# A piece of the projections between the second and the third group of turned probabilities

## The reference

```
h = rmsnorm(x, norm_g)
proj = h @ w_in
ya = forgetting_attention(qa, ka, va, log_f) * silu(za)   # 8 heads, causal
yb = dsa_attention(qb, k, v, q_idx, k_idx, w_idx) * silu(zb)   # 8 heads, top 256 keys
yc = dilated_attention(qc, kc, vc) * silu(zc)   # 12 heads, short windows
merged = sigmoid(ga) * (ya @ w_a) + sigmoid(gb) * (yb @ w_b) + sigmoid(gc) * (yc @ w_c)
out = rmsnorm(x + merged @ w_o)
```

## Time and profile before

| what | value |
|---|---|
| median of 3 runs | 1521.58 us (1520.7 to 1522.74) |
| the profiled execution: time, span | 1528.18 us, 1526.2 us |
| TensorE busy | 1440.7 us, 94% of the span |
| VectorE, ScalarE busy | 727.6 us (48%), 695.9 us (46%) |
| DMA | mean 63 GB/s |
| granted clock of TensorE, mean | 0.982 |
| stage A (steps a0.0 to a3.7) | from 725.9 us in the span |
| stage B (steps b0.0 to b3.7) | from 972.3 us to about 1235 us |

### The profile page before, as it was taken

How to read it: one execution, slowest core, us unless ns; L and a number is a source line. 1 busy time by engine, 2 the same in 40 slices (tenths; PEclk the granted TensorE clock), 3 DMA queues, 4 the chain that set the end, 5 groups by cost and what they waited for, 6 DMA issues and landing times.

```text
span 1526.2 us, 20911 instructions
## 1 busy us (share of the span) xinstructions
PE 1440.7 (94%) x7890; PEld 1132.0 (74%) x7890; DVE 727.6 (48%) x1568; ACT 695.9 (46%) x1482; POOL 64.8 (4%) x133
## 2 busy tenths in 40 slices
PE   4978899999999999999999999999999999999898
PEld 3756667777776778887777777777777778888686
DVE  5363865545565894555434334543333346232524
ACT  6253666656675452111555565454544433211412
POOL 1102210000000000000000000100000000000000
PEclk9987999999999999999999999999999999999999
DMA  5115511111111112222111000312222221222422
GB/s 169 26 30 136 132 50 34 35 35 29 35 35 36 35 42 62 76 76 76 43 29 28 22 22 15 117 49 52 88 70 73 87 84 42 69 83 83 145 83 97
DMA packets 112131, 96.58 MB, mean 63 GB/s; under 512 B 10528, under 2 KB 97952, under 8 KB 111776
## 3 DMA queue, kind: packets, MB, share of 16 engines
q1 hardware_dynamic: 100816, 58.54, 14.4%
q0 software_dynamic: 11216, 36.71, 7.7%
HBM read 72.95 MB, written 18.09 MB: 60 GB/s over the span
## 4 chain that ended last, share of the span: by engine, by line
PE 86%; DVE 6%; ACT 4%; issue 2%; DMA 1%; SPq 1%; DVEq 0%; ACTq 0%; POOL 0%; POOLq 0%
PE bank L750 21%; PE bank L752 21%; PE bank L751 20%; PE bank L928 6%; PE bank L909 6%; PE slot L900 4%; PE slot L885 2%; DVE idle_out L1336 1%; PE slot L750 1%; PE slot L752 1%; PE slot L751 1%; ACT pta L1189 1%; DVE score L1477 1%; ACT relu_t L1122 1%; ACT ptb L1189 1%
## 5 line engine op out<-in xcount | busy, mean ns | idle before, releaser
L750 PE MATMUL bank<-hs,w_hl 128*128 128x512 f32 x1152 | 463.9, 403 | 9.6 <-DVE tm L1582 5.5
L752 PE MATMUL bank<-hs,w_hl 128*128 128x512 f32 x1152 | 452.6, 393 | 0.0
L751 PE MATMUL bank<-hs,w_hl 128*128 128x512 f32 x1152 | 452.0, 392 | 0.0
L1309 DVE TENSOR_TENSOR w_hl<-w_raw,w_hl 128x512 fp32r<-128x512 f32 (+1 forms) x176 | 118.9, 679 | 355.9 <-ACT w_hl L1019 353.8
L750 PEld LDWEIGHTS bank<-hs,w_hl 128*128 128x128 f32 x1152 | 218.7, 190 | 55.8 <-issue 9.9
L752 PEld LDWEIGHTS bank<-hs,w_hl 128*128 128x128 f32 x1152 | 218.0, 189 | 47.6
L751 PEld LDWEIGHTS bank<-hs,w_hl 128*128 128x128 f32 x1152 | 218.7, 190 | 43.8 <-issue 0.8
L1019 ACT ACTIVATE w_hl<-w_raw 128x512 fp32r<-128x512 f32 (+1 forms) x176 | 109.1, 622 | 196.5 <-PE bank L752 186.6
L1336 DVE TENSOR_SCALAR_CACHE_REDUCE idle_out<-score,state 128x768 uint8<-128x768 f32 (+3 forms) x140 | 115.3, 824 | 4.8
L1207 ACT ACTIVATE idle_out<-score,state 128x896 bf16<-128x896 f32 x64 | 70.3, 1098 | 17.1 <-DVE state L1332 16.0
L1495 DVE CUSTOM_DVE_ANT_0 slot<-slot,score 128x128 f32<-128x128 f32 (+7 forms) x64 | 47.3, 781 | 46.1 <-PE slot L900 46.1
(11 more groups left out here) (297 smaller groups left out, 2115.8 us busy)
## 6 DMA issues: line engine op xcount, KB each, us to landing
w_raw<-in_w_in_dram SPq DMA_DIRECT2D x142, 256.0 KB, 2.8
merged_scratch<-ms POOLq DMA_DIRECT2D x16, 512.0 KB, 3.5
ms<-merged_scratch POOLq DMA_DIRECT2D x16, 512.0 KB, 4.1
xn<-in_x_dram SPq DMA_DIRECT2D x8, 512.0 KB, 6.6
iq_st<-iq_hl POOLq DMA_DIRECT2D x32, 128.0 KB, 2.6
qb<-qb_scratch POOLq DMA_DIRECT2D x8, 512.0 KB, 4.7
w_raw<-in_w_o_dram SPq DMA_DIRECT2D x16, 256.0 KB, 3.7
qb_scratch<-bq_high POOLq DMA_DIRECT2D x4, 512.0 KB, 3.0
```

The costliest lines, as they stand in the source:

```text
L750: pe.matmul(out_, wh, mh, start=start, stop=False)
L751: pe.matmul(out_, wh, ml, start=False, stop=False)
L752: return pe.matmul(out_, wl, mh, start=False, stop=stop)
L1309: v.tensor_tensor(lo, src, hi.bitcast(F32), ALU.subtract).then_inc(w_low, 1)
```

## The change

A step whose turned unit has more than two groups gets its `turn` in two parts, and one piece of the projections stands between them, if the step may have one. The number of pieces for a step is fixed ahead of the turning and what is left of it after the piece between is pumped where all of it was pumped before. Banks of the ring are handed out in the same order as before.

```diff
@@ -182,6 +182,11 @@
         for s in range(n + 2):
             for f in before.get(s, []):
                 f()
+            x = units[min(s, n - 1)]
+            if x["br"] == "a" and x["ch"] == NCH["a"] - 1:
+                pieces = 1 if x["b"] >= 4 else 0
+            else:
+                pieces = 2 * rate
             if s < n:
                 x = units[s]
                 x["slots"] = 2 if x["W"] > HALF else 1
@@ -198,16 +203,17 @@
                 for g0 in range(0, len(parts), 4):
                     x["groups"].append(dict(use=ring(), tp=nxt("tp"), parts=parts[g0:g0 + 4]))
                     unit_of_tp.append(x)
-                plan.append(("turn", x))
+                plan.append(("turn", dict(x, groups=x["groups"][:2])))
+                if len(x["groups"]) > 2:
+                    if pieces >= 1:
+                        pump(1)
+                        pieces -= 1
+                    plan.append(("turn", dict(x, groups=x["groups"][2:])))
             if s < n:
                 plan.append(("exp", units[s]))
                 if units[s]["br"] == "c" and s % 2 == 1:
                     pick()
-            x = units[min(s, n - 1)]
-            if x["br"] == "a" and x["ch"] == NCH["a"] - 1:
-                pump(1 if x["b"] >= 4 else 0)
-            else:
-                pump(2 * rate)
+            pump(pieces)
             flush_later()
         defer[0] = False
```

## The result

The changed kernel takes 1550.9 us in the median of four runs, against 1522.2 us for the kernel before; the ratio is 1.0177, 95% interval 1.0138 to 1.0216. Medians here take in the one slow run each that the changed kernel (2384.5 us) and e3 (1629.4 us) had, without which they are 1550.0 and 1512.0 us; the ratios leave such runs out. So the changed kernel is 1.8% slower, some 27 to 29 us. The forecast was 1549 us, slower. Why it is slower was forecast too; of the two sizes that make it up, one was too large and one too small.

A forecast was written before the change was run, and what follows sets the result against it. TensorE, on 86% of the chain that ended last, was taken to bound the kernel. Stalls and switching less waits saved, +19.3 us, and clock falls, +8.5 us, made +28 us: median 1549 us from 1521.6, range 1537 to 1560.

The forecast's parts named there:

- The wait that goes: TensorE's third group of transpositions no longer waits for ScalarE's copy: 0.48 us saved in 30 steps, 14.4 us.
- The split itself: TensorE changing to and from a piece between groups: adds 0.20 us with another piece behind, 0.10 us without.
- the first sum: Stages A and B at unchanged clock: waits saved, switching costs and new stalls together make +19.3 us.
- The cover lost: In 16 steps no piece stays behind the last group, so exponentials are uncovered; 11 stalls of 2.0 to 2.8 us.
- 14 with a piece behind: Steps of stages A and B keeping a piece after the last group: no stall, -0.28 us each, -3.9 us.
- a0.5, a1.5, a2.5: Stage A, pairs 0 to 2, issuing block 5's logits and turning block 4: stall 2.0 us, +5.2 us together.
- a3.6, b0.6: Stage A pair 3 and stage B pair 0, block 6's logits: stall 2.8 us, +2.45 us each, +4.9 together.
- a0.7, a1.7, a2.7, b1.7: Block 7's logits, stage A pairs 0 to 2, stage B pair 1: stall 1.96 us, +1.6 each, +6.4 together.
- The clock: TensorE's clock halves after half of 11 new stalls: 5.5 falls at 1.55 us each, +8.5 us.
- Rival 1: New stalls stay hidden, so the change gains the removed copy waits less switching: -10 us, 1512 us; chance 5%.
- Rival 2: Every new stall brings a clock fall: 1558 us; 9 or more falls, 1554 to 1561 us; chance 20%.
- Rival 3: Hardly any clock fall at the new stalls, 0 to 2: 1538 to 1545 us; chance 22%.

The follow-up runs named there:

- e3: Against the kernel before: two pieces dealt to each step turning a wide block, one of them between the groups, fewer pieces elsewhere; 1512.4 us, ratio 0.9923.
- e2: Changed kernel, but a piece goes between only in 15 steps where no other stays behind the turning; 1555.2 us, ratio 1.0219 to the kernel before.
- e5: Changed kernel, but the weight split of a piece between stands behind the exponentials in ScalarE's queue; 1548.8 us, ratio 1.0175 to the kernel before.
- e6: Changed kernel, but in the 16 steps with nothing behind, half a piece stands between and half behind; 1519.7 us, ratio 0.9970 to the kernel before.
- e8: Changed kernel with 6 or 4 extra, overwritten matmuls in each of the 11 stalls; 1541.0 us, ratio 1.0106 to the kernel before.
- e1: Changed kernel, but a piece goes between only in the 14 steps where another stays behind; 1518.3 us, ratio 0.9971 to the kernel before.

## Why the prediction was right, step by step

**The wait that goes**: 0.48 us forecast, in 30 steps. Its entries left the list, as said, but for one. It was a little more: turning block 5 takes 0.86 + 0.36 us now against 1.75 before (a1.6, a0.6), so 0.53.

**The split itself**: 0.20 us where a piece is between and another behind. Too much. From the piece to the third group it is 2.84 to 2.86 us against 2.73 for a piece within a run of pieces, so the change from the piece back to the transpositions costs 0.11 to 0.13, and the change from them to the next piece costs nothing that wasn't there. Thirteen of the 14 steps gained 0.38 to 0.51 us each, not 0.28, the last turning of B 0.3: -6.3 instead of -3.9 us. That is the largest error of the first sum.

**The cover lost**: confirmed, in place and number. By step (the last turning of B stands in the first row; b3.0 and b3.1 together, since a piece went from one to the other), changed less before, falls taken out at 1.55 each:

| steps | forecast | trace |
|---|---|---|
| 14 with a piece behind | -3.9 | -6.3 (13 of them -6.0) |
| a0.5, a1.5, a2.5 | +5.2 | +4.9 |
| a3.5, b2.5 | +4.0 | +3.7 |
| a3.6, b0.6 | +4.9 | +4.9 |
| a0.7, a1.7, a2.7, b1.7 | +6.4 | +5.9 |
| a1.0, a2.0 and the steps behind them | +0.7 | +0.3 |
| a3.7 | +1.0 | +1.0 |
| b3.0 with b3.1 | 0 | 0.0 |
| b3.7 | +1.0 | +0.8 |
| all (added up unrounded) | +19.3 | +15.3 |

The chain "third group, copies, exponentials, logits" was read off single steps of the kernel before, and held: 2.74 us in .7 (forecast 2.71), a stall of 1.93 (1.96). The other stalls were 2.00 (2.0), 2.24 (2.37) and 2.67 us (2.8). e2 puts the whole loss on these steps, e5 excludes the weight split, and e6 shows that work put back behind the last group comes off the stall one to one.

**The clock**: forecast 5.5 falls, 8.5 us; in the profiled execution 8, 12.4 us. The price (1.55) was right for a fall of 3.4 us; the two that lasted twice as long cost about 2.8. That about half of such stalls bring a fall was a guess from two rows; in the three kernels that have the same eleven stalls it was 8 (changed), 5 (e2) and 6 (e5). Taking the stalls' idle time apart (e8) gave back 11 us in the timed runs. The first sum was 4 us too high and this one 3.9 too low, so that the total came out so close is luck; each part alone was off by a quarter to a third of what was measured.

**Rival 1** (stalls hidden) fell: that the logits need banks which the exponentials hold is the wait in the list. It describes e3 well, where the cover is kept: -11.7 us. **Rival 2** (every stall a fall, 9 or more) fell, if by one fall only: a0.6 began after 2.00 us of idle time at full clock. The sentence of the Trainium skill ("TensorE: Matmul & The Clock Gate", section "A second HAM failure mode: psum-queue depth-cycling") on small idle times making the clock swing is borne out here in part: idle times of 1.9 to 2.7 us had a fall in 19 of 33 cases in the three traces, those of 0.5 to 1.3 us in e6 in none of 11. **Rival 3** (hardly any fall) fell in all three traces.

## What to carry to other kernels

Work that fills one wait is taken from another place, where it may have hidden something longer: before moving it, follow the queue of the engine that is behind it (here ScalarE, 2.6 to 3.3 us from the third group to the logits that wait for its exponentials) and count the steps in which nothing else covers that. The same idea applied only where cover stays, with the filler work dealt to the steps that need it (e3), gave -12 us instead of +29. On TensorE a stall of 2 us cost more than itself here, since the clock could fall with it; four or six useless matmuls in it were cheaper than idling (e8: 11 us).

## What was not expected of the hardware

With the same eleven stalls of 1.9 to 2.7 us in three kernels (one trace of each), the clock fell at 8, 5 and 6 of them, not always the same ones, and at none of eleven of 0.5 to 1.3 us. Even a stall that brought a fall in the nine other traces (2.08 us ahead of a3.4) brought none in e6. What decides between a stall of 2 us with a fall and one without isn't shown. Most falls lasted 3.4 us and cost about 1.55 us; two lasted 6.8 us (a3.4 in e1, a3.7 in e2) and cost about 2.8.
